# The first norm beside the first modulation sums, bias rows behind the second half's norm, value matrices a stage ahead

## What is computed

```python
# first block, layer 0: the condition vector makes shift, scale and gate
c_act = silu(c)
mod = c_act @ ada_w[l] + ada_b[l]
sh1, sc1, g1, sh2, sc2, g2 = split(mod, 6)
hn = modulate(rms_norm(h, norm_mix_g[l]), sh1, sc1)   # xn*(1+scale)+shift
mix = hgrn2_mixer(hn, hgrn_w_in[l], ...)              # hn @ w_in, 1024 x 4096
...
# third block: norm, one projection of 3792 columns, two mixers
h = rmsnorm(x, g_pre) * (1 + scale) + shift
qkv_a, z_a, b_a, a_a, q_b, ckv, z_b, iq, ik, iw = split(h @ w_in, ...)
# sparse attention: index scores choose the keys, then
ckv = rmsnorm(ckv, g_kv)
logits = q_b . ckv * R_KV**-0.5 + rel_bias[t5_bucket(dist)]
o = softmax(logits) @ ckv
o = einsum('blhr,hrd->blhd', o, w_uv) * silu(z_b)
```

## Time and profile before

| | us |
|---|---|
| median of three runs | 2551.88 |
| lowest and highest run | 2547.09, 2552.87 |
| the profiled execution, device time | 2549.29 |
| its span, first to last instruction | 2546.8 |
| TensorE busy in it | 2015.5 |
| VectorE busy | 1651.5 |
| ScalarE busy | 795.7 |
| GpSimd busy | 661.3 |
| mean granted TensorE clock (share of 2.4 GHz) | 0.895 |

### The profile page before, as it was taken

How to read it: one execution, slowest core, us unless ns; L and a number is a source line. 1 busy time by engine, 2 the same in 40 slices (tenths; PEclk the granted TensorE clock), 3 DMA queues, 4 the chain that set the end, 5 groups by cost and what they waited for, 6 DMA issues and landing times. The chain is left out here.

```text
span 2546.8 us, 31885 instructions
## 1 busy us (share of the span) xinstructions
PE 2015.5 (79%) x11958; PEld 1317.7 (52%) x11958; DVE 1651.5 (65%) x3778; ACT 795.7 (31%) x1783; POOL 661.3 (26%) x657
## 2 busy tenths in 40 slices
PE   2999978697776798789698778859887678756886
PEld 2888868463331365454265456415333266636664
DVE  5668876588787776545768666587974417844442
ACT  1112221234423424532434553253222231231221
POOL 1222100233434333433333343343344200000000
PEclk9999989798987899899799898978899879877889
DMA  8997751399999999999899798999999823110000
GB/s 315 347 382 297 265 219 67 121 419 414 370 421 421 416 419 415 421 403 396 321 393 366 297 366 344 378 398 369 419 420 419 334 100 102 66 73 1 9 9 17
DMA packets 124682, 746.74 MB, mean 293 GB/s; under 512 B 13536, under 2 KB 16480, under 8 KB 56304
## 3 DMA queue, kind: packets, MB, share of 16 engines
q0 software_dynamic: 93792, 610.66, 59.9%
q1 hardware_dynamic: 30736, 134.05, 13.6%
HBM read 741.25 MB, written 3.41 MB: 292 GB/s over the span
## 5 line engine op out<-in xcount | busy, mean ns | idle before, releaser
L1670 POOL DMA_INDIRECT got<-in_peer_uv,idx x512 | 586.1, 1145 | 951.4 <-PE ps L1640 803.0
L1640 PE MATMUL ps<-got,diag 64*64 64x512 f32 x3936 | 601.5, 698 | 285.6 <-ACT diag L1727 264.5
L1764 DVE CUSTOM_DVE_ANT_0 got<-got,xk 128x1024 f32<-128x1024 f32 x512 | 616.9, 1222 | 258.9 <-DMA got<-in_peer_uv,idx 249.0
L1640 PEld LDWEIGHTS ps<-got,diag 64*64 64x64 f32 x3936 | 118.1, 144 | 560.6 <-ACT diag L1727 458.3
L1722 ACT ACTIVATE gelu<-eye,hid 128x64 f32<-128x64 f32 x492 | 169.9, 345 | 659.2 <-DVE hid L1764 651.8
L1229 PE MATMUL ps<-xT,ring 128*128 128x256 f32 x928 | 225.1, 394 | 6.6 <-DVE qkv L1318 6.6
L1229 PEld LDWEIGHTS ps<-xT,ring 128*128 128x128 f32 x928 | 174.6, 194 | 85.7 <-issue 48.5
L931 PE MATMUL ps<-xT,ring 128*128 128x256 f32 x768 | 187.2, 393 | 1.7 <-ACT xT L1044 1.7
L1727 ACT ACTIVATE diag<-gelu,gate 128x64 f32<-128x64 f32 x492 | 171.1, 348 | 52.1 <-PE ps L1640 6.7
L931 PEld LDWEIGHTS ps<-xT,ring 128*128 128x128 f32 x768 | 142.2, 192 | 75.5 <-issue 45.9
L192 POOL DMA_DIRECT2D vring<-in_vslabs x136 | 72.4, 533 | 278.9 <-DVE in_b_psums L304 137.5
(11 more groups left out here) (565 smaller groups left out, 2598.0 us busy)
## 6 DMA issues: line engine op xcount, KB each, us to landing
ring<-in_small SPq DMA_DIRECT2D x158, 512.0 KB
vring<-in_vslabs POOLq DMA_DIRECT2D x136, 512.0 KB, 6.0
ring<-in_slabs SPq DMA_DIRECT2D x18, 2048.0 KB, 10.5
got<-in_peer_uv,idx POOLq DMA_INDIRECT x512
h<-in_x SPq DMA_DIRECT2D x2, 2048.0 KB, 8.1
w_out<-in_slabs SPq DMA_DIRECT2D x2, 2048.0 KB, 10.5
out<-h SPq DMA_DIRECT2D x4, 512.0 KB, 2.6
bias_rows<-brow POOLq DMA_DIRECT2D x1, 1280.0 KB, 4.8
```

The costliest lines, as they stand in the source:

```text
L1640: mm = nc.tensor.matmul(ps[to:to + HALF, i, :], diag[own, d % NDIAG, :], got[own, n % GRING, 1, 512 * g:512 * g + 512], start=(k == 0), st ...
L1670: nc.gpsimd.indirect_dma_start(out=got[:, n % GRING].rearrange("p a d -> p (a d)"), out_offset=None, in_=table, in_offset=bass.IndirectOff ...
L1764: nc.vector.tensor_tensor_reduce(row_in, row_in, xk[:, w % 2, :], 1.0, 0.0, ALU.mult, ALU.add, hid[:, w % 2, k:k + 1]).then_inc(dotted, 1)
```

## The change

Three edits.

1. `first_mods` takes the place of `project("mods_a", ...)` and `norm_to_xT("n0", ...)`: one block for both. ScalarE takes all four squares (into `rows[:, 0, :]`), the root behind VectorE's eighth slab, and the scaling of the four tiles; TensorE transposes seven of the eight channel tiles behind the sums of the third group and the last one when `mod` is written (bank 7 holds the sums until then). The writes of `xT` are split as before.
2. In `second_half` the bias products move from ahead of step 0 to behind steps 14 to 17 (`BROW`), the copy of the gate row from step 0 to 12, the copies of the bias rows to steps 15 to 18, and `GATE_A` from 14 to 19.
3. `w_uv` is allotted a level further out, and its load is the first on SP's queue in `second_half`. `sparse` still waits on the same semaphore.

```diff
+    def first_mods(nv, xn):
...
+                @block.tensor
+                def _(pe):
+                    def turn(k):
+                        for t in range(NT):
+                            if k == 0:
+                                pe.wait_ge(scaled, t + 1)
+                            mm = nc.tensor.transpose(ps[:, k, P * t:P * t + P], xn[:, t, P * k:P * k + P], ident)
+                        mm.then_inc(turned, 1)
+
+                    groups = nv // PIECES
+                    for m in range(groups):
+                        pe.wait_ge(part_sum, ND * (m + 1))
+                        for j in range(VCOLS // P):
+                            col = (VCOLS // P) * m + j
+                            mm = nc.tensor.matmul(ps[:, 7, col:col + 1], psums[:, m % NPART, P * j:P * j + P], ones[:, 0:1],
+                                                  start=True, stop=True)
+                        mm.then_inc(vector_done, 1)
+                        if m == groups - 2:
+                            for k in range(ND - 1):
+                                turn(k)
+                    pe.wait_ge(mods_taken, 1)
+                    turn(ND - 1)
+
+                @block.scalar
+                def _(act):
+                    for t in range(NT):
+                        if t:
+                            act.wait_ge(squared, t)
+                        nc.scalar.activation(sq, h[:, t, :], ACT.Square, accum_out=ss[:, t:t + 1]).then_inc(squared, 1)
+                    root(act, 0, ss[:], root_in, root_mid, root_out)
+                    act.wait_ge(root_out, 1)
+                    for t in range(NT):
+                        nc.scalar.activation(xn[:, t, :], h[:, t, :], ACT.Copy, scale=ss[:, t:t + 1]).then_inc(scaled, 1)
+                    act.wait_ge(norm_ready, 1)
+                    for k in range(0, ND, 2):
+                        act.wait_ge(turned, k + 1)
+                        nc.scalar.activation(xT[:, k, :], ps[:, k, :], ACT.Identity, bias=shift[:, k:k + 1], scale=norm_a[:, k:k + 1])
+
+                @block.vector
...
+                        if m == 7:
+                            dve.wait_ge(squared, NT)
+                            ve.tensor_scalar(ss[:], ss[:], 1.0 / D, EPS, ALU.mult, ALU.add).then_inc(root_in, 1)
+                    dve.wait_ge(vector_done, nv // PIECES)
+                    ve.tensor_tensor(mod[:, 0:16], ps[:, 7, 0:16], v("bias", 0, 16), ALU.add).then_inc(mods_taken, 1)
+                    dve.wait_ge(mods_taken, 1)
+                    step(ve.tensor_scalar(norm_a[:], scale, 1.0, None, ALU.add))
+                    ve.tensor_tensor(norm_a[:], norm_a[:], v("mix_g", 0, 8), ALU.mult).then_inc(norm_ready, 1)
+                    dve.wait_ge(norm_ready, 1)
+                    for k in range(1, ND, 2):
+                        dve.wait_ge(turned, k + 1)
+                        ve.tensor_scalar(xT[:, k, :], ps[:, k, :], norm_a[:, k:k + 1], shift[:, k:k + 1], ALU.mult, ALU.add)
...
-            SQUARE, MEAN, NORM, TURN, TURNED, GATE_A, GATE_QKV = 20, 22, 24, 25, 27, 14, 56
-            PIECE = 30
+            SQUARE, MEAN, NORM, TURN, TURNED, GATE_A, GATE_QKV = 20, 22, 24, 25, 27, 19, 56
+            PIECE, BROW = 30, 14
...
                     sp.sem_inc(frow_seen, 16)
+                    sp.dma_start(w_uv[:], io["w_uv_2"][0].rearrange("h r d -> r h d")).then_inc(uv_loaded, 16)
                     sp.dma_start(gain_b[:, 0:136], io["rowvec"][0:1, D:D + 136].broadcast_to([P, 136])).then_inc(row_loaded, 16)
...
-                    pe.wait_ge(wide_ready, 1)
-                    for a in range(HB):
-                        if a % 2 == 0:
-                            pe.wait_ge(brow_out, 2 * a) if a else pe.wait_ge(gp_out, 1)
-                        for g in range(2):
-                            mm = nc.tensor.matmul(ps[:, 2 * (a % 2) + g, 0:ZR // 2], rwide[:, a],
-                                                  hot[:, ZR // 2 * g:ZR // 2 * (g + 1)], start=True, stop=True)
-                        mm.then_inc(brow_done, 1)
                     for s, _ in enumerate(side["pe"](pe)):
+                        if BROW <= s < BROW + HB:
+                            a = s - BROW
+                            if a == 0:
+                                pe.wait_ge(wide_ready, 1)
+                            if a % 2 == 0:
+                                pe.wait_ge(brow_out, 2 * a) if a else pe.wait_ge(gp_out, 1)
+                            for g in range(2):
+                                mm = nc.tensor.matmul(ps[:, 2 * (a % 2) + g, 0:ZR // 2], rwide[:, a],
+                                                      hot[:, ZR // 2 * g:ZR // 2 * (g + 1)], start=True, stop=True)
+                            mm.then_inc(brow_done, 1)
...
-                        if s == 0:
+                        if s == BROW - 2:
                             act.wait_ge(summed, 1)
                             nc.scalar.activation(gp_row[:], ps[:, 0:2, :].rearrange("p a b -> p (a b)"), ACT.Copy).then_inc(gp_out, 1)
-                            for a in range(HB):
-                                act.wait_ge(brow_done, a + 1)
...
+                        if BROW < s <= BROW + HB:
+                            a = s - BROW - 1
+                            act.wait_ge(brow_done, a + 1)
...
                 @block.sync
                 def _(sp):
-                    sp.dma_start(w_uv[:], io["w_uv_2"][0].rearrange("h r d -> r h d")).then_inc(loaded, 16)
                     sp.wait_ge(loaded, 16)
...
-            project("mods_a", [], range(first), take_mods(0, 16))
-            norm_to_xT("n0", [(xT, v("mix_g", 0, 8), mod[:, 8:16], mod[:, 0:8])], work=g_all)
+            first_mods(first, g_all)
```

## The result

The change makes the kernel faster: 2541.34 us (median of 20 runs, 2526.36 to 2553.99) against 2554.39 (20 runs, 2547.09 to 2562.79). The ratio is 0.9944 with a 95% interval of 0.9933 to 0.9956, that is 14.3 us less, between 11.2 and 17.1. The direction was right and the time lies in the range, at its top; the forecast gain of 19.6 was too large by 5.

A forecast was written before the change was run, and what follows sets the result against it. TensorE is busy for 2015.5 of 2546.8 us, so only gaps that every engine sits through can be won, in three places. -9.2 - 7.6 - 2.8 = -19.6 from 2549.29 or 2551.88, taken as 2531; range 2524 to 2542.

The forecast's parts named there:

- The first term, -9.2: Start: first norm beside the modulation sums; projection starts 10.2 us earlier, less 1 for TensorE's clock; ends -12.4 and -5.
- time won ahead of this stage stays won if the loads keep up: First projection stage, 61 to 182 us: TensorE is busy for 121.00 of 121, so an earlier start is kept.
- Rival 3: Start: slabs under way until 60 us bound the stage, TensorE waits at first vector sums, nothing won; 2541 us, chance 0.06.
- The second term, -7.6: Second half's start: bias rows behind the norm remove 12.3 us, added products cost 4.4, w_uv's load 0.3; ends -11.5 and -1.1.
- the same 6 us pass at 1.2 GHz whichever work fills them: Second half: TensorE's clock recovers some 8.5 us after jobs begin, as before, so added bias products cost +4.4 us.
- the prediction's own sign of being wrong, shorter by less than 4: Second half: wrong if the stage from the root to VectorE's last search row shortens by less than 4 us.
- Rival 2: Half-speed work: added bias products and first projection jobs run at 1.2 GHz; sum -9, about 2542 us, chance 0.12.
- The moved silus: Second half: compressed keys' norm finished by 2085.6, asked for at 2086.2; half a microsecond of slack, no stall counted.
- the rule: Second half, ScalarE: a drain of about 1.38 us per table switch would make the sum 2.2 us smaller.
- The third term, -2.8: Sparse attention's start: with w_uv loaded a stage ahead, TensorE's first product starts with the block; ends -2 and -2.9.
- Its last sign of being wrong: Whole kernel: wrong if something outside the three changed places moves by more than 3 us.
- rival 4: First projection: late slabs make TensorE wait repeatedly and drop to 1.2 GHz; ten slow jobs give 2565 us, chance 0.02.

The follow-up runs named there:

- paced slabs: The change with 128-row bias products and the first projection slab asked for at the start, the second after 16 pieces, the third after 24; ratio 0.9924 to the kernel before.
- early slab: The change with the first projection slab asked for at the start of the first block's sums, not after 24 pieces; ratio 0.9923 to the kernel before.
- 128 rows with the early slab: The change with bias products padded to 128 rows and the first projection slab asked for at the start; 2528.99 against 2557.37 us before, ratio 0.9885.
- the first edit alone: Only first_mods put into the kernel before, nothing else; ratio 0.9974, 6.6 us less.
- the edits one by one: Three runs, each with one of the three edits in the kernel before; ratios 0.9974, 0.9980 and 1.0001 in the order of the edits.
- the edit alone: Only the load of w_uv moved a block ahead in the kernel before; ratio 1.0001 (0.9986 to 1.0017).

## Why the prediction was right in direction and too high in size

**The first term, -9.2.** Its steps up to the projection's start were right, and a little cautious: over the six profiles with the change's own loads and groups in that block (all but the early and paced slabs) it starts 10.9 us earlier on average (42.5 over the three without the edit, 31.6 with it). The cost of the slow first jobs was there: 16.27 us for the 64 rows that took 14.05, 2.2 where I took 1. What failed is the condition in "time won ahead of this stage stays won if the loads keep up". The working behind it took only the first and third projection slabs and the first group of vector slabs, found 1.5 us of slack, and stopped. The loads kept up there, and fell behind further on. Counted to the end of the stage the gain is 4.8 us (166.8 to 162.0, leaving out the kernels with other slabs or groups), and 4.4 at the load of `h`. The earlier trace rows had the warning: with a share of 0.93 over 121 us the DMA engines had 8.5 us to spare at the most, less than the 10 us by which I started the stage ahead of them. The rates come nearer to what was kept: 357 GB/s for 121 us are 43.2 MB, and at the 369 GB/s that the change's profile reaches they take an estimated 117, that is 4 us less. The early slab bears it out from the other side: between 17 and 36 us the change leaves the DMA engines a share of 0.72, and with the slab there it is 0.91,

```profile
17.00:36.00 19.00, 3.88 (x17) 3.71 (x17) 17.34 (x26) 11.84 (x16) 5.82 (x11) 1.00 0.72 249
```

```profile
17.00:36.00 19.00, 3.73 (x16) 3.56 (x16) 15.63 (x23) 10.25 (x15) 5.29 (x10) 1.00 0.91 342
```

(the first window is the change's, the second that of 128 rows with the early slab), and the gain at the load of `h` becomes 9.6 us (346.6 to 336.9, three kernels each): the size that I had forecast. It is an average of few profiles, 336.2 to 338.2 with the early slab and 338.3 to 345.1 without. Rival 3 was the right mechanism, at half its price: not the first vector sums wait but the last.

**The second term, -7.6.** The removed 12.3 us are right: jobs start 12.2 earlier in the block (30.8 to 18.6, over three and five kernels). The 30.8 holds a dear one: the first edit alone has 32.2, with the clock at 1.2 GHz during all eight bias products, for 30.0 and 30.2; without it the jobs start 11.5 earlier. The added work was mis-sized. I took +4.4 and it is 9.0 on average (26.0 to 35.0, over the five profiles with 32-row products in that place, from 33.3 to 38.2). The failed step is "the same 6 us pass at 1.2 GHz whichever work fills them". It does matter which. With the products over 32 rows there, 2.4 GHz came back after 12.2 to 22.8 us in five profiles; over 128 rows after 8.9 to 9.8 in three; and with none of them there after 8.5 to 10.4 in five. No profile with 32-row products there lies among the other eight, while the other two kinds can't be told apart. How long the delay is varies from one execution to the next: the change had 22.8 and 12.2 us. The fast price was low as well, 0.64 a product rather than 0.55, 5.1 for eight; the slow one was 1.2. The gain of the edit in its block is 3.3 us on average (2.5 without that dear one) instead of 7.6, and nothing in the one execution profiled after the change: from `gp` to VectorE's last search row it took 176.2 us there, 175.5 before and 171.5 in the change's second profile, so that the prediction's own sign of being wrong, shorter by less than 4, was met in the first and just missed in the second. Rival 2 (half-speed work) named this at a chance of 0.12, with -1.1 for this term; 3.3 is nearer to that than to 7.6. Its sum of -9 is near the stages' sum below partly by luck, since it put the loss at the start down to the clock and not to the loads.

**The moved silus.** The estimate of when the norm is finished against when it is asked for held: 2088.72 against 2091.8, no stall, and 3.1 us of room where I gave half a microsecond. Slow products are not the reason: the room is 2.9 in the three profiles with 128 rows, where all pairs but the first were fast. From the start of the square to the finished norm it took 4.1 us (2084.64 to 2088.72) and not the 6.6 carried over from before. The sum by rows was right here and the rule would have misled: a table load of 1.28 at 2078.78 is followed by the silus at 2080.07, 1.29 later. The drain that the Trainium skill adds (ScalarE: Activation LUTs, "What ACT_TABLE_LOAD costs") does not show in this trace.

**The third term, -2.8.** 2.9 in every profile with the edit. The time of the edit alone does not resolve it.

**The sum.** -4.4 - 3.3 - 2.9 makes -10.6 by the stages, the edits one by one make -11.4 by time, and the change as a whole -14.3 (11.2 to 17.1) and -19.7 (12.8 to 26.6) in its two measurements. These agree within their widths; what lies between 11 and 14, or 20, is not settled, and the spread of the gathers and of the last block can hold it. So the time lies in the stated range, near its upper end, while the three stages account for 10.6 of the 14.3 us: the prediction can't claim the rest. Its last sign of being wrong, something else moving by more than 3 us, can't be read from single profiles, since the last block moved by 4.5 between two profiles of one kernel. Two small sums in it are off: rival 2 gives 2540 to 2543, and rival 4 passes plus 0.2% only after eight slow jobs. Rival 4, slower, was never near.

## What to carry to other kernels

Before a stage is counted as keeping the time won ahead of it, multiply the idle share of its DMA engines by its length: count no more than that as kept. Here it was less still, 4.8 us of 8.5. Work that is moved in beside narrow products is to be priced at TensorE's lower clock unless a trace shows the higher one with *that* work in it; here it helped to put it among wide products over all 128 rows, or to pad it. When a gain vanishes between two stages, count both from a mark inside the program, since one execution's total moves by more than the gain.

## What the runs showed of the hardware

Padding with 96 rows of zeros made the bias products cheaper as a whole: over 32 rows three of their four pairs took about 2.5 us in the change's first profile, and in the other four profiles the first pair took 2.50 and the second 1.47 to 1.79; with 128 rows the first took 2.48 and the others 1.24, because the clock had risen. While the clock was at 1.2 GHz a pair cost the same with either number of rows (2.50 and 2.48). TensorE was busy for all of the windows shown at 0.50 and for the one at 0.98; in these its busy time does not tell the clock. Why rows count, the runs don't show.

The five vector slabs of 512 KB asked for just behind the three projection slabs took 11.5 to 20.4 us to land before the change and 12.0 to 20.7 after it; the eleven asked for ahead of them took 3.7 to 5.5 and 3.6 to 5.9. A 2 MB slab asked for 18 us earlier cost VectorE 1.6 us of waiting, and the second one asked for 6 us earlier as well brought this to 10.3.
